# Moving a selection load, eight small matmuls and one input table in the opening of a two-block network kernel

## The reference

```python
c_act = jax.nn.silu(c)
mods = c_act @ w_ada[i] + b_ada[i]
sh1, sc1, g1, sh2, sc2, g2 = [...]
h = modulate(rms_norm(x, norm1_g[i]), sh1, sc1)      # h * (1 + scale) + shift
u = h.astype(f32).reshape(bsz, seqlen, SSM_GROUPS, SSM_GROUP)
...
bbar_re = qr[..., None] * br - qi[..., None] * bim
bbar_im = qr[..., None] * bim + qi[..., None] * br
bu_re = jnp.einsum('blgh,gph->blgp', u, bbar_re)
bu_im = jnp.einsum('blgh,gph->blgp', u, bbar_im)
_, _, xr, xi = lax.associative_scan(_ssm_combine, (a_r, a_i, bu_re, bu_im), axis=1)
y = (jnp.einsum('ghp,blgp->blgh', c_re, xr) - jnp.einsum('ghp,blgp->blgh', c_im, xi))
```

## Time and profile before

| | us |
|---|---|
| median of 3 runs | 2669.48 |
| lowest and highest run | 2668.41, 2672.12 |
| span of the profiled execution, first to last instruction | 2666.9 |
| PE busy in it | 2622.2 |
| DVE busy in it | 1473.0 |
| ACT busy in it | 1050.9 |
| first L630 (start of the S5 loop's steady part) | 52.56 |

### The profile page before, as it was taken

The page is one execution under the profiler, slowest core; times in us unless marked ns, Lnnn a source line. Parts: engine busy times, 40 slices in busy tenths (PEclk is TensorE's granted clock), DMA queues, the critical chain, the costliest instruction groups (busy, mean ns, idle before and its releaser), DMA issues.

```text
span 2666.9 us, 38062 instructions
## 1 busy us (share of the span) xinstructions
PE 2622.2 (98%) x15896; PEld 2214.3 (83%) x15896; DVE 1473.0 (55%) x2185; ACT 1050.9 (39%) x1495; POOL 116.9 (4%) x150
## 2 busy tenths in 40 slices
PE   6999999999999999999999999999999999999998
PEld 3689888888898888888888888988888988988887
DVE  8967555565563333465555555844336777833335
ACT  4535222233242222255555555523223665522323
POOL 7610000000000000000000000000000000000000
PEclk8999999999999999999999999999999999999999
DMA  6084555423322222222222222132222122232220
GB/s 244 2 307 167 196 191 189 182 72 95 111 95 98 101 104 101 87 72 74 80 74 72 73 80 82 57 126 95 95 95 80 56 87 95 79 111 95 95 95 32
DMA packets 46246, 282.89 MB, mean 106 GB/s; under 512 B 6129, under 2 KB 8561, under 8 KB 20098
## 3 DMA queue, kind: packets, MB, share of 16 engines
q1 hardware_dynamic: 40146, 238.02, 26.0%
q0 software_dynamic: 5936, 42.51, 4.3%
HBM read 278.41 MB, written 2.10 MB: 105 GB/s over the span
## 4 chain that ended last, share of the span: by engine, by line
PE 85%; DVE 9%; ACT 3%; DMA 2%; issue 1%; SPq 0%; POOL 0%; DVEq 0%; ACTq 0%
PE PS L672 17%; PE PS L674 17%; PE PS L673 17%; PE PS L807 4%; PE PS L809 4%; PE PS L808 4%; PE PS L896 2%; PE PS L644 1%; PE PS L765 1%; PE PS L764 1%; PE PS L763 1%; PE PS L836 1%; PE PS L837 1%; PE PS L838 1%; DMA adab<-adaw 1%; PE PS L884 1%
## 5 line engine op out<-in xcount | busy, mean ns | idle before, releaser
L672 PE MATMUL PS<-Hl,Wh 128*128 128x512 f32 x1256 | 488.9, 389 | 0.8 <-DVE Wl L1618 0.7
L673 PE MATMUL PS<-Hh,Wl 128*128 128x512 f32 x1256 | 488.6, 389 | 0.0
L674 PE MATMUL PS<-Hh,Wh 128*128 128x512 f32 x1256 | 488.6, 389 | 0.0
L1174 ACT CAST Wh<-raw 128x2048 fp32r<-128x2048 f32 (+2 forms) x156 | 281.3, 1848 | 401.5 <-PE PS L674 380.7
L1618 DVE TENSOR_TENSOR Wl<-raw,Wh 128x2048 fp32r<-128x2048 f32 (+2 forms) x160 | 347.0, 2208 | 67.0 <-ACT Wh L1174 66.7
L672 PE MATMUL PS<-Gl,Wh 128*128 128x512 f32 x880 | 342.4, 389 | 0.0
L674 PE MATMUL PS<-Gh,Wh 128*128 128x512 f32 x880 | 342.3, 389 | 0.0
L673 PE MATMUL PS<-Gh,Wl 128*128 128x512 f32 x880 | 342.3, 389 | 0.0
L672 PEld LDWEIGHTS PS<-Hl,Wh 128*128 128x128 f32 x1256 | 235.8, 188 | 50.1 <-DVE Wl L1618 1.4
L673 PEld LDWEIGHTS PS<-Hh,Wl 128*128 128x128 f32 x1256 | 235.8, 188 | 48.9
L674 PEld LDWEIGHTS PS<-Hh,Wh 128*128 128x128 f32 x1256 | 235.8, 188 | 48.9
(11 more groups left out here) (464 smaller groups left out, 4787.4 us busy)
## 6 DMA issues: line engine op xcount, KB each, us to landing
raw<-wstream SPq DMA_DIRECT2D x152, 1024.0 KB, 6.2
raw<-wstream SPq DMA_DIRECT2D x64, 768.0 KB, 4.5
adab<-adaw POOLq DMA_DIRECT2D x40, 1024.0 KB, 5.5
raw<-wstream SPq DMA_DIRECT2D x20, 512.0 KB, 3.7
raw<-adap SPq DMA_DIRECT2D x4, 1024.0 KB, 10.9
ada_land<-adap SPq DMA_DIRECT2D x4, 1024.0 KB, 19.0
X<-xT SPq DMA_DIRECT2D x1, 2048.0 KB, 8.3
XU<-xU SPq DMA_DIRECT2D x1, 1536.0 KB, 15.5
```

What stands on the lines that cost most here:

```text
L672: mm(o, Wh[:, s, c0:c0 + P], xl[:, k, :], start=k == 0, stop=False)
L673: mm(o, Wl[:, s, c0:c0 + P], xh[:, k, :], start=False, stop=False)
L674: last = mm(o, Wh[:, s, c0:c0 + P], xh[:, k, :], start=False, stop=k == kt - 1)
L1174: nc.scalar.copy(w_high(p, h, widths[h]), raw[:, h, 0:widths[h]]).then_inc(split_h, 1)
```

## The change

It does five things. SP loads JS third, with a semaphore of its own (`js_in`), and no more with the six small tables. PE does the eight products with JS in front of piece 5 instead of piece 6. DVE makes the modulation factors and `s5_u(0)` first, and `s5_f1(1)` only then. The copy QPP moves from DVE to ACT, where it waits for DVE's last doubling and first two inputs ("dbl") and for POOL's coefficients ("tab"). DVE waits for that copy ("qpp") behind `s5_states(0)`.

```diff
         def _(sp):
             sp.dma_start(S5A[:, :, :], s5a).then_inc(s5a_in, 16)
             sp.dma_start(cs[:, :], cC).then_inc(c_in, 16)
+            sp.dma_start(JS[:, :, :], jsel).then_inc(js_in, 16)
             sp.dma_start(X[:, :, :], xT).then_inc(x_in, 16)
...
-                             (S5D[:, :], s5d), (GS[:, :], gsel), (JS[:, :, :], jsel)):
+                             (S5D[:, :], s5d), (GS[:, :], gsel)):
                 sp.dma_start(dst, src).then_inc(consts_in, 16)
...
-                if k == N_ADA_PE - 2:
-                    pe.wait_ge(consts_in, 16 * 6)
+                if k == N_ADA_PE - 3:
+                    pe.wait_ge(js_in, 16)
                     pe.wait_ge(s5_s["rn"], 1)
...
             s5_u(0)
+            act.wait_ge(s5_s["dbl"], 1)
+            act.wait_ge(s5_s["tab"], 1)
+            nc.scalar.copy(QPP[:, :, :, :], QP[:, :, :, 8:32]).then_inc(s5_s["qpp"], 1)
             s5_uu(1)
...
             s5_uu(0)
-            s5_f1(1)
-
-            dve.wait_ge(consts_in, 16 * 6)
+
+            dve.wait_ge(consts_in, 16 * 5)
             dve.wait_ge(s5_s["col"], 1)
...
             s5_u(0)
+            s5_f1(1)
             double(5, 16, 32)
-            link(V_.tensor_copy(QPP[:, :, :, :], QP[:, :, :, 8:32]))
             s5_uu(1)
+            dve.wait_ge(s5_s["xu"], 2)
+            dve.sem_inc(s5_s["dbl"], 1)
             dve.wait_ge(rho_done, 1)
             s5_states(0)
+            dve.wait_ge(s5_s["qpp"], 1)
             for t in range(KT):
```

More of the change, by code:

```diff
@@ L277, in build @@
         ada_pe, rho_done = sem("ada_pe"), sem("rho_done")
-        x_in = sem("x_in")
+        x_in, js_in = sem("x_in"), sem("js_in")
         xu_in, xu2_in = sem("xu_in"), sem("xu2_in")
@@ L326, in build @@
             "fir", "mods", "cact", "ab", "sel", "rn", "ru", "abu", "tab", "e", "f", "tr", "ftc", "kx", "kf", "inc",
-            "xin", "inter", "yi", "y", "gh", "gl", "xr", "us", "xu", "u", "f1", "row", "col", "rnp", "bb", "nc", "prm_a", "prm_v", "rot1")}
+            "xin", "inter", "yi", "y", "gh", "gl", "xr", "us", "xu", "u", "f1", "row", "col", "rnp", "bb", "nc", "prm_a", "prm_v", "rot1", "dbl", "qpp")}
         lb_diff, lb_done = sem("lb_diff"), sem("lb_done")
```

## The result

| | before | after |
|---|---|---|
| median of 20 runs each, side by side, us | 2668.61 | 2672.10 |
| lowest and highest, us | 2665.40, 2673.84 | 2669.57, 2675.34 |
| span of the profiled execution | 2666.9 | 2668.6 |
| start of the first L630 (L631 after) | 52.56 | 55.82 |
| its length | 1.96 | 3.32 |

The ratio is 1.0014, with a 95% interval of 1.0008 to 1.0021: 3.5 us slower by the medians. The executions of one kernel differ by 6 to 8 us among each other, so one execution decides nothing here.

A forecast was written before the change was run, and what follows sets the result against it. It took PE and DVE both to bound the opening before the first L630. −1.2 (sums) +3.7 (`s5_f1(1)`) −0.6 (QPP) +0.1 (wait) = +2.0, plus 1.8 (clock) = +3.8: 2673.3 us, range 2669.0 to 2677.0.

The forecast's parts named there:

- DVE is a bound as well as PE: Before u_s: DVE is full until the factors, so a step freeing PE alone leaves DVE waiting; no size.
- the table: `s5_f1(1)` on DVE, moved behind u_s; claimed to cost +3.7 us there.
- JS third delays pieces 6 and 7 by 0.5: SP's load queue: later issues come 0.5 us later, so pieces 6 and 7 land at 31.7 and 34.1.
- The sums end 1.2 earlier, not 3.6, as piece 7's landing limits them: PE's sums: end at 35.95 instead of 37.18, −1.2 us, because PE must wait for piece 7.
- The path to u_s stays 4.2 long; u_s at 40.2: From the sums through ACT, L565, transposes and L612 to u_s: length unchanged at 4.2 us.
- rival B: Factors' path: clock also low from L565 through L612, +2.0 us more, total +5.8, 2675.3 us; 25%.
- `s5_f1(1)` behind u_s, +3.7, bounds 2.0 to 4.2: DVE's chain after u_s: the instructions stand there in full at their old price, +3.7 us.
- QPP −0.6, the wait behind the second input +0.1: DVE before the states: moving the copy saves 0.6 us, waiting for `s5_uu(1)` to end costs 0.1.
- L630 starts at 1.2 GHz, +1.8: PE at the loop's start: a hole of 4.7 us leaves the clock at half, +1.8 us, bounds 0 to 5.1.
- Total: Whole kernel: states' start +2.0 us plus clock +1.8 gives +3.8 us, time 2673.3 us.

The follow-up runs named there:

- Kernel 1: The kernel before with JS loaded third and its products in front of piece 5, nothing else: 2668.31 us, ratio 1.0001.
- 4: The kernel before with only `s5_f1(1)` moved behind u_s: 2673.76 us, ratio 1.0022.
- Kernel 2: The kernel before with only the copy QPP moved to ACT, with its waits: 2669.50 us, ratio 1.0004.
- 5: The changed kernel with five products of constants in PE's holes in front of the first L631: 2670.66 us, ratio 1.0007.
- 7: The changed kernel with `s5_f1(1)` back in its old place and ACT copying the coefficients of tiles 0 and 1 into PS early: 2666.91 us, ratio 0.9997.
- 3: The changed kernel with `s5_f1(1)` back in its old place, in front of the modulation factors: 2666.54 us, ratio 0.9995.
- 10: Kernel 7 once more, the same program: 2669.21 us, ratio 1.0002.
- 9: Kernel 8 with three instead of two products of constants in front of the second transposes and one more behind them: 2666.04 us, ratio 0.9992.
- 8: Kernel 7 with eleven products of constants on PE's path and two more in front of the second transposes: 2666.53 us, ratio 0.9995.
- kernel 11: Kernel 9 with the first load of `wstream` held until piece 7 is summed: 2665.92 us, ratio 0.9994.
- 12: Kernel 9 again, the same program: 2666.00 us, ratio 0.9994.

## Why the prediction was right, point by point

Forecast was +3.8 us (2673.3); measured +3.5 by the medians, 2672.1. The direction, the cause and the size (within 0.2%) are right. That the medians come so near is in part luck, as the last point says. By its steps:

- **DVE is a bound as well as PE.** Right, and the step that carries the case. Kernel 1 frees PE alone and gains nothing; 4 moves the table alone and loses 5.6.
- **JS third delays pieces 6 and 7 by 0.5.** Wrong in its reason. SP had put out the last small table by 15.3 and issues piece 6 only when PE is done with the first piece in `raw`; it did so at 21.27 before and at 21.28 after, so nothing of JS's issue reached it. Kernel 2, with JS in its old place, has 22.15. Piece 7 still landed 0.3 later than before, at 33.92; no run shows why. SP's queue after:

```profile
21.28 1.19 SPq L462 DMA_DIRECT2D raw<-adap  x2
```

- **The sums end 1.2 earlier, not 3.6, as piece 7's landing limits them.** Right in the place and the reason: 35.95, with the expected wait for `raw` in front. But the 1.2 is not all the change's: kernels 2 and 4 end at 35.89 and 36.07 with the products in the old place. I took a low clock of one execution (piece 5 in 1.93 us) for a property of the kernel.
- **The path to u_s stays 4.2 long; u_s at 40.2.** Not in the changed kernel's profile: 6.0 long, u_s at 41.95, because the clock was at half throughout. With all of it at the full clock, as in kernel 4, it is 4.1 long and u_s starts at 40.14: the step was sized right for that state of the clock. (5 and 7, at 40.35 and 40.34, have a full clock in the columns and a lower one in the second transposes, 1.09 and 0.75.) This is rival B, to which I gave 25%; it came true in this execution. As 2 and 3 show it needs neither JS's new place nor the table's, and as 7 and 10 show one program has it in one execution and not in another; so it can't be counted as a sure cost of the change. How often each kernel has it, no run tells. B's own price, +2.0, came out as +1.79.
- **`s5_f1(1)` behind u_s, +3.7, bounds 2.0 to 4.2.** Mis-sized in the profile: +2.89. The first product met POOL between two instructions (0.71), the second did not (1.59). In 4 it is 3.7. So the price does depend on where POOL stands, as the bounds said; the old place's price was the upper part of it.
- **QPP −0.6, the wait behind the second input +0.1.** −0.59; +0.29 for the stretch from the second input's start to the states. The copy is hidden, with 1.3 us between the end of the transposes and L631.
- **L630 starts at 1.2 GHz, +1.8.** Right in kind, 1.36 in size: the clock came back before the end of L631. Kernel 4 has 3.68 for 1.96, and after it 1.82 for 1.15 at L605. Kernel 5 shows that the hole is the cause, and 9 against 8 shows it again (1.96 for 2.96).
- **Total.** The states' start is 3.25 later and not 2.0, because of the path; with the clock, 4.6 in the profile against 3.8. The medians give 3.5. Against the working the profile has the path +1.8, the table −0.8, the wait behind the second input +0.2 and the clock −0.4, so the errors cancel in part, and the nearness of 3.8 to 3.5 is no proof of the single terms. Executions with a full clock in the path, as in 5 and 7, would have 1.6 less, and a mixture of the two gives what was measured. That is argued: one execution of the changed kernel was profiled.

The Trainium skill (TensorE: Matmul & The Clock Gate, "HAM oscillation") says that bursts of matmuls between waits for DMAs start cold each time. The hole before L631 is a wait for DVE and not for a DMA, and the clock fell there too (3.32 for 1.96). For the path with its waits for DMAs the rows agree in some executions only: 1.87 in 2, 3 and 10, 1.06 in 1, 4 and 7, with the same wait for `raw` in 1, 3, 7 and 10.

## What to carry to other kernels

Where two engines reach a meeting point together, freeing one gives nothing, and work taken from before the meeting point to behind it is paid in full, though each list looks better sorted: look at what the engine does in the idle time that the other leaves it. A DVE product with two SBUF operands beside a busy POOL is worth a small early copy of one of them into PSUM (3.7 to 2.0 us here), but only when the other bound goes down with it. And where differences are a tenth of a per cent, read mechanisms from the profiles' lines and sizes from medians of ten runs or more; the spans of two profiled executions said 1.7 where the runs say 3.5. Even such medians differed by 2.3 us, against their own runs of before, for one program (7 and 10).

## What the runs showed of the hardware that was not expected

**The clock can be low while PE is busy without a pause.** In kernel 11 it fell at about 31.0 after two stretches with PE busy 3.40 of 3.40 and 3.60 of 3.60 us (windows of kernel 11, columns as above):

```profile
24.00:27.40 3.40, 3.40 (x24) 0.96 (x16) 1.74 (x4) 3.40 (x4) 3.14 (x5) 1.00 1.04 399
27.40:31.00 3.60, 3.60 (x29) 2.38 (x26) 3.12 (x5) 0.28 (x2) 3.36 (x4) 0.99 1.03 407
31.00:32.00 1.00, 1.00 (x3) 0.53 (x2) 0.93 (x4) 0.00 (x0) 0.92 (x2) 0.50 1.10 451
```

What had run there were sums with 32 columns of weights and the JS products of one row, between a few full products; in kernels 9 and 12 the same list of work, with the same busy times of 3.40 and 3.60 in these two stretches, still had a PEclk of 1.00 from 31.00 to 32.00. A stretch that the profile shows as wholly busy is therefore no assurance of the full clock behind it, and why it fell is open.

**Late clock falls hide the difference of the spans.** In the profile before, the clock was at half at the norm between the blocks; after the change, at the same place of the program, it was not (windows of before, then of after):

```profile
1149.00:1152.00 3.00, 3.00 (x16) 3.00 (x16) 3.00 (x5) 1.29 (x2) 0.00 (x0) 0.50 0.00 0
```

```profile
1153.00:1156.00 3.00, 3.00 (x28) 3.00 (x27) 3.00 (x6) 1.85 (x3) 0.00 (x0) 1.00 0.05 18
```

The shift between the two kernels is 4.6 us up to there and 3.0 behind it, and another 1.3 go between 2086 and 2095 us, where the execution before waited longer for a load; the latter was not followed further. The change touches neither place; whether the shift of 4.6 us itself has a part in them is not shown.
